# Decoder step with a mixture of experts, one core: gate weights loaded in two pieces, final norm's weights moved behind tile rows, one expert buffer's load split around a gather

## The reference, cut to what matters

```python
y = _moe(_rmsnorm(x, norm_ffn_g).reshape(B * T, -1), router_w, router_bias,
         ex_w1, ex_w3, ex_w2, sh_w1, sh_w3, sh_w2).reshape(B, T, -1)
x = x + y
gate = jax.nn.sigmoid(jnp.einsum('btd,de->bte', _rmsnorm(x, norm_ple_g), w_ple_gate))
x = x + jnp.einsum('btp,pd->btd', p, w_ple_proj) * gate
...
y_prompt = _rmsnorm(xp, final_norm_g)
y_sample = _rmsnorm(xs, final_norm_g)
```

## Time and profile before

| | us |
|---|---|
| median of 3 runs | 989.14 |
| lowest and highest | 988.08, 989.21 |
| the profiled execution | 987.02 |
| its span, first to last instruction | 985.3 |

### The profile page before, as it was taken

How to read it: one execution, slowest core, us unless ns; L and a number is a source line. 1 busy time by engine, 2 the same in 40 slices (tenths; PEclk the granted TensorE clock), 3 DMA queues, 4 the chain that set the end, 5 groups by cost and what they waited for, 6 DMA issues and landing times.

```text
span 985.3 us, 16443 instructions
## 1 busy us (share of the span) xinstructions
PE 931.7 (95%) x6050; PEld 422.5 (43%) x6050; DVE 518.5 (53%) x1281; ACT 151.4 (15%) x371; POOL 360.7 (37%) x451
## 2 busy tenths in 40 slices
PE   7999999999999999999999998989988999999996
PEld 6777878745544332232232332323322233333442
DVE  5766754447777444535445443444442445452885
ACT  3011134300112111111111110101100111113322
POOL 6303532201266344434454433434432444441131
PEclk9999999999999999999999998989999999999999
DMA  8212230621697999999999999999999999988932
GB/s 294 87 30 90 85 105 10 236 96 64 196 375 307 348 382 410 414 408 414 412 412 413 413 413 414 399 399 402 412 408 392 366 413 411 412 331 342 423 119 85
DMA packets 75532, 299.10 MB, mean 304 GB/s; under 512 B 14650, under 2 KB 26114, under 8 KB 48309
## 3 DMA queue, kind: packets, MB, share of 16 engines
q1 hardware_dynamic: 59549, 260.26, 67.0%
q0 software_dynamic: 15904, 37.79, 10.0%
HBM read 278.13 MB, written 31.50 MB: 314 GB/s over the span
## 4 chain that ended last, share of the span: by engine, by line
PE 58%; DMA 20%; DVE 9%; issue 7%; POOL 4%; DVEq 1%; POOLq 0%; SPq 0%; ACT 0%; ACTq 0%
PE bank L2773 19%; PE bank L2358 18%; DMA arena<-xs_dram,slot 9%; DMA arena<-in_ex_w 6%; PE bank L2768 6%; PE bank L2877 6%; DMA ring<-in_ex_w 3%; POOL arena L1083 3%; PE bank L2364 2%; PE bank L2616 1%; POOL arena L975 1%; DVE x L2261 1%; PE bank L2530 1%; PE bank L2519 1%; DMA y_dram<-arena,outrow 1%
## 5 line engine op out<-in xcount | busy, mean ns | idle before, releaser
L2773 PE MATMUL bank<-arena 128*32 128x512 f32 x1440 | 272.5, 613 | 8.3 <-issue 4.8
L1083 POOL DMA_INDIRECT arena<-xs_dram,slot x192 | 201.6, 1050 | 68.5 <-issue 58.5
L2773 PE MATMUL bank<-ring,arena 128*32 128x512 f32 x864 | 214.0, 610 | 4.0 <-DMA arena<-in_ex_w 4.0
L1099 POOL DMA_INDIRECT y_dram<-arena,outrow x46 | 47.2, 1027 | 275.4 <-DVE slot L2105 228.0
L2119 DVE STREAM_TRANSPOSE arena<-arena 128x1024 f32<-128x1024 f32 x48 | 99.3, 2068 | 84.5 <-DMA arena<-xs_dram,slot 84.4
L2773 PE MATMUL bank<-xT,arena 128*32 128x512 f32 x576 | 115.4, 607 | 4.7 <-DMA ring<-in_ex_w 4.7
L2773 PEld LDWEIGHTS bank<-arena 128*32 128x32 f32 x1440 | 68.0, 112 | 111.2 <-issue 105.4
L2198 DVE COPY outrow<-yrow 128x1 int32<-128x1 int32 x46 | 7.1, 154 | 148.0 <-PE bank L2773 119.8
L2773 PE MATMUL bank<-mixpj,arena 128*32 128x512 f32 x384 | 84.7, 594 | 0.0
L2773 PEld LDWEIGHTS bank<-ring,arena 128*32 128x32 f32 x864 | 51.0, 112 | 49.0 <-issue 44.1
L1344 ACT ACTIVATE arena<-bank 128x256 f32<-128x256 f32 x46 | 17.7, 385 | 340.7 <-PE bank L2773 258.1
(11 more groups left out here) (470 smaller groups left out, 1394.1 us busy)
## 6 DMA issues: line engine op xcount, KB each, us to landing
arena<-in_ex_w SPq DMA_DIRECT2D x78, 1024.0 KB, 20.8
ring<-in_ex_w SPq DMA_DIRECT2D x50, 1024.0 KB, 22.5
xT<-in_ex_w SPq DMA_DIRECT2D x28, 1024.0 KB, 17.7
mixpj<-in_ex_w SPq DMA_DIRECT2D x24, 1024.0 KB, 19.1
arena<-y_dram SPq DMA_DIRECT2D x18, 1024.0 KB, 12.0
wide<-in_ex_w SPq DMA_DIRECT2D x12, 1024.0 KB, 24.4
ring<-in_w_in SPq DMA_DIRECT2D x4, 2048.0 KB, 8.4
ring<-in_w_out SPq DMA_DIRECT2D x2, 2048.0 KB, 11.1
```

The source lines that it names most:

```text
L1083: pool.indirect_dma_start(xg[b][:, 256 * a:256 * a + 256], None, xs_quarter, bass.IndirectOffsetOnAxis(slot[k][:, a:a + 1], 0), bounds_che ...
L1099: pool.indirect_dma_start(y_dram, bass.IndirectOffsetOnAxis(outrow[b][:, 0:1], 0), og[b], None, bounds_check=K * T - 1, oob_is_err=False). ...
L2773: ins = pe.matmul(b[t, :], lhs[:, t], rhs(home(own if lane < 3 else common)), start=start, stop=stop)
```

## The change

It makes five edits. (a) The first load of home 3 is split: w1 as before, w3 only after the second gather (`s_gather[1]` at 64) has landed; w2 and the shared expert's w2 stand behind w3. (b) `gt0` is loaded in two pieces of 1 MB, the first (which overwrites home 0's w2) after mm2 of step 43, the second after mm2 of step 44, on a semaphore of its own, `s_gt0`. (c) The load of the final norm's weights moves from right after the last mm2 to behind the four loads of tile 0's outputs. (d) DVE waits for them before the first `final` and not before the first `add_up`. (e) `ysum` moves ahead of the projection half of tile 3 on PE, and their banks change places.

```diff
-    g += [(("pj", tail[4], 0), "s"), (("ysum",), "v")] + norm3(0)
+    g += [(("ysum",), "v"), (("pj", tail[4], 0), "s")] + norm3(0)
...
-            def load13(k, e):
-                for w, src in enumerate((ex_w1, ex_w3)):
+            def load13(k, e, which=(0, 1)):
+                for w in which:
+                    src = (ex_w1, ex_w3)[w]
...
             for p in (1, 2, 4, 3):
                 if home(p) == 3:
                     after(sp, "sh", NP_ - 1)
-                load13(home(p), NE - 1 - p)
+                if home(p) == 3:
+                    load13(3, NE - 1 - p, (0,))
+                    sp.wait_ge(s_gather[1], 64)
+                    load13(3, NE - 1 - p, (1,))
+                else:
+                    load13(home(p), NE - 1 - p)
                 load2(home(p), NE - 1 - p)
...
             load_chunk("gt1")
-            sp.wait_ge(s_mm2, more * STEPS + (max(final[0], final[1]) + 1))
-            load_chunk("gt0")
-            sp.wait_ge(s_mm2, more * STEPS + STEPS)
-            sp.dma_start(g_b[:, :], bc(final_norm_g)).then_inc(s_gb, 16)
+            wgt = chunk("gt0").rearrange("p (c n) -> p c n", n=512)
+            rows = w_ple_gate[0].rearrange("(c p) n -> p c n", p=P)[:, :, 0:512]
+            for k in range(2):
+                sp.wait_ge(s_mm2, more * STEPS + (final[k] + 1))
+                sp.dma_start(wgt[:, 4 * k:4 * k + 4], rows[:, 4 * k:4 * k + 4]).then_inc(s_gt0, 16)
...
+                if a == 1:
+                    sp.wait_ge(s_mm2, passes * STEPS)
+                    sp.dma_start(g_b[:, :], bc(final_norm_g)).then_inc(s_gb, 16)
...
+                if a == 0:
+                    dve.wait_ge(s_gb, 32)
                 dve.wait_ge(s_rstdf, a + 1)
...
             dve.wait_ge(s_ga, 32)
-            dve.wait_ge(s_gb, 32)
             add_up(0)
...
+            ysum()
             pj_half(TAIL[4], 0)
-            ysum()
             norm3(0)
             pj_half(TAIL[4], 1)
+            pe.wait_ge(s_gt0, 32)
+            chunk_in(pe, "gt1")
             for n in range(2):
-                chunk_in(pe, f"gt{n}")
                 wait_drained(pe, "x3T", NP_, n)
```

More of the change, by code:

```diff
@@ L507, in decoder_step @@
         s_y8 = [[sem(f"s_y8_{b}{q}") for q in range(4)] for b in range(2)]
-        s_pj, s_xsum = sem("s_pj"), sem("s_xsum")
+        s_pj, s_xsum, s_gt0 = sem("s_pj"), sem("s_xsum"), sem("s_gt0")
         s_ys = [sem("s_ys0"), sem("s_ys1")]
```

## The result

| | us |
|---|---|
| changed kernel, median of 20 runs | 990.47 (988.41 to 992.66) |
| kernel before, 20 runs beside them | 988.53 (986.61 to 990.68) |
| ratio, 95% interval | 1.0019 (1.0012 to 1.0025) |
| profiled execution after, and its span | 990.17, 988.4 |
| the same for before | 987.02, 985.3 |

The change made the kernel slower by 1.9 us, just under the 0.2% that I had called no change; I had forecast a gain of 0.7. The number lies in my range, but the sign is wrong, and so is a reason; that it lies in the range is owed to the range's width.

What follows compares the result with a forecast made beforehand. It took one engine at a time to bound the tail, PE with its gathers and the weight stream the loop. Terms -0.8 + 0.5 - 1.3 + 0.8 + 0.1 = -0.7 gave 988.4 us against 989.14; range 985.6 to 991.4.

Steps and rivals of the forecast that it cites:

- Edit a: Expert loop, split load of home 3: second gather lands earlier, the weight stream gains; -0.8 us, bounds -3.1 to +1.8.
- the lead of 3.1 us: PE before step 1: hole shorter by 1.4 us, and 1.7 us saved if the clock doesn't fall.
- the wait for weights at 644: Expert loop: PE stands 4.01 us for a weight load; there it keeps the stream's lead, not its own.
- the stream: Weight loads in the loop: 2.7 us of later idle time filled less 1.9 us of new idle, 0.8 us ahead.
- nothing else moves: SP's queue: home 0's refill isn't issued before about 315.8 us anyway, after the held loads go at 313.0.
- rival 4: Second gather: the load's queue doesn't matter to it, so edit a only costs, +1.8 us, 991.0 in all; chance 0.05.
- Edit b's last gather: Loop's end: beside the first gate piece the last gather takes 5.7 us, not 5.19; +0.5, bounds 0 to +2.9.
- Rival 3: Loop's end: first gate piece delays the last gather to 8.1 us; 990.8, or 992.1 without scatter gain; chance 0.13.
- The last scatter: Tail, edits b and c: less load in its way, lands in 6.1 us, not 7.44; -1.3, bounds 0 to -2.
- Edit c's collision: Tail: norm's 0.5 MB ahead of tile 1's loads makes them 1.25 us later; +0.8, bounds 0 to +1.3.
- Edit e: PE's order in the tail: the moved half fills a 1.65 us hole and is longer by 0.1; +0.1.
- Edit d: DVE's wait for the final norm's weights: it ended before the sample tile's sum anyway; 0.

Runs made afterwards that it cites:

- The control: The kernel before, unchanged, run in the place of an experiment and profiled a second time: 988.32 us, ratio 1.0002.
- the longer hold: Home 3's w3 held until the third gather, on the kernel before: ratios 1.0001, 1.0011; on the changed kernel, norm's load behind tile 2's rows: 1.0003.
- e12_hold13: Kernel before with both halves of home 3's first load, and all behind them, held until the third gather landed: 992.95 us, ratio 1.0047.
- e5_bce: Kernel before with edits b to e, all but the split load: 988.30 us, ratio 1.0003.
- c5_c: Repeat of edits c and d alone on the kernel before, norm's weights behind tile 0's loads: 989.67 us, ratio 1.0010.

## Why the prediction was wrong

**Edit a, -0.8 predicted, +0.9 measured (two runs alone, 1.0011 and 1.0007).** This is the step that failed, in three places. Both intervals leave out the predicted gain (0.9992); neither is clear of nothing by itself.

First, the lead of 3.1 us. I made it 1.4 us from the hole and 1.7 from the clock. The control shows the clock's part as the chance of an execution: it fell in three of nine. The hole's part is real and came as worked out (0.48 or 0.49 in all five profiles with edit a). The landing of 4.6 us that I took came too: issued at 309.76, waited for until 314.37.

Second, I looked for what is late next and stopped at the wait for weights at 644. The next late thing was the third gather, one step on, which I never costed though its wait of 2.32 us stands at 320.91, just behind the rows that I read. POOL issues it at its old time and it lands no sooner, so PE can't turn to the third step's one-hot matrices sooner either. It does so 9.3 to 9.7 us after the first silu in the six profiles without the split whose clock stayed up, 9.5 to 10.3 with edit a, and 8.7 to 8.9 with the longer hold, where this gather too is early. PE comes to that place about 0.9 us sooner than in those six and stands 1.0 to 1.8 there: the lead, and up to 0.9 more. From the first to the third silu edit a brings nothing: 22.9 against 22.8, and against 22.4 where the clock had stayed up anyway.

Third, the stream, which I had ahead by 0.8 us. I had a new idle time of 1.9 us, and 2.7 us later on into which the held loads would flow. Over all profiles the share from 308 to 328 us is 0.90 with edit a and 0.95 without the split, 1.1 us of new idle time; from 328 to 362 it is 0.95 and 0.93, which fills 0.7 of them and not all. In that stretch SP waits for homes to come free, and with PE no further on than before they come free no sooner. So the stream is 0.4 to 0.5 us behind (352 GB/s against 355 over the 54 us say the same), in place of 0.8 ahead. I had also said that nothing else moves: home 0's refill goes off 0.6 to 1.0 us behind the first silu with edit a, before 0.1. The run with both halves held shows that a long enough debt reaches PE. That this small one makes edit a's 0.9 is not shown: with the longer hold, whose debt is larger by the share, it was +0.1 and +1.1. Where in the loop the 0.9 us are lost stays open; shown is that PE's lead ended at the third gather.

What the Trainium skill says in "DMA: Bandwidth & Descriptors", section "Queues, rings and completion order", that an engine serves its queues in turn, packet by packet, I had drawn on for rival 4, with 0.05. The rows go against what I made of it: from the issue of the second gather's last part until DVE goes on it took 6.7 to 7.2 us with four loads beside it (nine profiles), 4.6 to 5.0 with one (eight), and at most 3.8 with none (e12_hold13, where DVE has no wait). So what stands in another queue does hold a gather up.

**Edit b's last gather, +0.5 predicted, 0 measured.** In the changed kernel DVE stood 0.17 us for PE's last mm2 ahead of its last copy and had no wait for the last gather; edit b alone gave 1.0003. In eight of the nine profiles with edit b the copy starts within 0.1 us of the end of that mm2, as without it; in e5_bce the gather makes it 0.35. Rival 3 did not come.

**The last scatter, -1.3 predicted, -0.7 measured.** It landed in 5.97 in the profile after, as I said. But over the profiles whose chain shows it, it took 6.9 to 7.4 with the norm's load ahead of it (mean of seven 7.2) and 6.0 to 6.9 without (mean of eight 6.5). I had set the longest of the first against the shortest of the second kind.

**Edit c's collision, +0.8 predicted, +0.9 measured.** PE's time from tile 0's transposes to tile 1's is 11.91 us in every profile without it, and 12.2 to 13.3 (mean of five 12.8) with it. It is the one term that was right in place and size, and it outweighs the scatter's true gain. Alone the edit costs 1.0 to 1.1 us in both timings, of which the mean tails show 0.6, and two of the five tails with it (98.1, after and c5_c) show none. The rest I can't place. The forecast had put the tail's two terms together at a gain of 0.5, and they came out at a loss of 0.2 on PE's and the scatter's rows.

**Edit e, +0.1 predicted.** The sample tile's transposes start 2.44 us after the start of its sum's last product in place of 2.24: +0.2. One thing more goes with the order that I had not seen. In the old one PE stands 1.65 us for DVE there, and in five of the ten profiles with it (both of edit c alone among them) the granted clock falls to its lower level for some 3 us near 910 us; tile 0's transposes then come 11.2 us after the sample tile's in place of 10.9. In the seven with edit e and a single norm load it never falls there. **Edit d:** 0, as said; no run has it alone.

The sum of the measured terms for a and c is 1.9, what the first comparison of the change gave; the second gave 0.9. My rival on the slower side was the wrong one: not the last gather but the sum of two small losses, in terms that I had as gains.

## What to carry to other kernels

When a wait is removed by holding a queue back, follow the next transfer of the kind that was protected, not only the next wait of the bound engine: here it was issued at its old time and landed no sooner, and the lead ended there. Put a load that nobody needs soon behind transfers whose readers have slack, not behind the first that happens to be convenient; here tile 2's rows in place of tile 0's took back 1.0 to 1.7 us. And before a term rests on one execution's stall or landing time, get a second profile of the unchanged kernel, or take the term from several instances of the same thing.

## What the hardware did that I had not expected

The granted clock fell to its lower level for some 3 us behind a hole of 1.5 to 1.8 us on PE (at 318 us) in three of nine executions, and stayed up in the other six behind holes of 1.4 to 1.7; behind holes of 0.5 there it never fell in nine.

ACT started the silu 0.1 us after the modelled end of its product in the first profile of before, and 1.5 to 2.0 us after it in most steps of all others, where the trace names the releaser "remote". PE's order of products was the same. Steps take 11.2 us in the one and about 11.6 in the other, and yet the whole loop is no longer. What sets it I don't know.

A load of 0.5 MB issued behind six of 1 MB on the same queue landed 16.4 us after its issue, and the same load with nothing ahead of it in 3.5 us, so a wait for it on SP in that place holds back everything behind it by the whole backlog.
